# Two blocks of a transformer on one core: modulation chunks reordered at the head of the weight stream, with the first query chunk taken two tiles at a time

## What is computed

```python
c_act = jax.nn.silu(c)
mod = c_act @ w_ada[l] + b_ada[l]
sh_m, sc_m, gt_m, sh_f, sc_f, gt_f = jnp.split(mod, 6, axis=-1)
h = modulate(rms_norm(x, g_mix[l]), sh_m, sc_m)      # h * (1 + sc_m) + sh_m
proj = jnp.einsum('bsd,de->bse', h, w_in[l])
```

## Time and profile before

| | us |
|---|---|
| median of 3 runs | 866.93 (864.98 to 868.29) |
| the profiled execution, its own time | 866.99 |
| its span, first to last instruction | 865.2 |
| TensorE busy | 790.4 (91%) |
| VectorE busy | 683.1 (79%) |
| ScalarE busy | 427.8 (49%) |
| GpSimd busy | 152.8 (18%) |
| mean granted TensorE clock | 0.973 of full speed |
| moved by DMA | 156.93 MB, mean 181 GB/s |

### The profile page before, as it was taken

The page is one execution under the profiler, slowest core; times in us unless marked ns, Lnnn a source line. Parts: engine busy times, 40 slices in busy tenths (PEclk is TensorE's granted clock), DMA queues, the critical chain, the costliest instruction groups (busy, mean ns, idle before and its releaser), DMA issues.

```text
span 865.2 us, 13446 instructions
## 1 busy us (share of the span) xinstructions
PE 790.4 (91%) x5495; PEld 719.0 (83%) x5496; DVE 683.1 (79%) x910; ACT 427.8 (49%) x604; POOL 152.8 (18%) x109
## 2 busy tenths in 40 slices
PE   0599999998989899999998999589979999999996
PEld 0499987886988899999998998468847899999995
DVE  3966477877877799999869899999966955796852
ACT  2444446453645744555445746564446144455652
POOL 0000011221000113211311009975530000000000
PEclk9799999999999999999999999889998999999998
DMA  9976787664745377667645260021220641473201
GB/s 351 401 269 253 276 291 297 228 236 175 240 163 195 107 282 249 241 227 261 248 188 213 81 237 16 40 84 62 67 80 22 236 154 49 172 295 118 98 2 48
DMA packets 26088, 156.93 MB, mean 181 GB/s; under 512 B 2691, under 2 KB 7084, under 8 KB 7852
## 3 DMA queue, kind: packets, MB, share of 16 engines
q1 hardware_dynamic: 21392, 148.91, 46.5%
q10 hardware_dynamic: 4636, 7.18, 2.7%
HBM read 155.01 MB, written 1.06 MB: 180 GB/s over the span
## 4 chain that ended last, share of the span: by engine, by line
PE 68%; DVE 20%; issue 5%; ACT 4%; ACTq 1%; DMA 1%; POOL 0%; DVEq 0%
PE wide L1230 27%; PE bank L1230 26%; DVE arena L1054 6%; DVE w_lo L814 5%; DVE w_lo L844 4%; ACT w_hi L372 2%; PE bank L1501 2%; PE bank L1265 1%; PE wide L1665 1%; PE bank L1641 1%; DMA raw<-in_w 1%; PE bank L1653 1%; PE wide L1329 1%; PE bank L1489 1%; PE bank L1351 1%
## 5 line engine op out<-in xcount | busy, mean ns | idle before, releaser
L844 DVE TENSOR_TENSOR w_lo<-raw,w_hi 128x2048 fp32r<-128x2048 f32 x93 | 215.4, 2318 | 68.1 <-ACT w_hi L372 66.5
L1230 PE MATMUL bank<-h_hi,w_hi 128*128 128x256 f32 x736 | 212.0, 288 | 12.0 <-DVE h_lo L880 9.7
L1230 PE MATMUL bank<-h_lo,w_hi 128*128 128x256 f32 x736 | 209.4, 285 | 0.0
L1230 PE MATMUL bank<-h_hi,w_lo 128*128 128x256 f32 x736 | 209.3, 284 | 0.0
L1230 PE MATMUL wide<-h_hi,w_hi 128*128 128x256 f32 (+1 forms) x576 | 189.2, 329 | 20.7 <-DVE w_lo L844 13.2
L1230 PE MATMUL wide<-h_lo,w_hi 128*128 128x256 f32 (+1 forms) x576 | 185.8, 323 | 0.0
L1230 PE MATMUL wide<-h_hi,w_lo 128*128 128x256 f32 (+1 forms) x576 | 185.7, 322 | 0.0
L372 ACT CAST w_hi<-raw 128x2048 fp32r<-128x2048 f32 x93 | 176.9, 1905 | 10.7 <-DMA raw<-in_w 4.7
L1230 PEld LDWEIGHTS bank<-h_hi,w_hi 128*128 128x128 f32 x736 | 142.2, 193 | 14.3 <-issue 11.3
L1230 PEld LDWEIGHTS bank<-h_lo,w_hi 128*128 128x128 f32 x736 | 142.4, 194 | 0.1
L1230 PEld LDWEIGHTS bank<-h_hi,w_lo 128*128 128x128 f32 x736 | 142.4, 193 | 0.0
(11 more groups left out here) (238 smaller groups left out, 1059.3 us busy)
## 6 DMA issues: line engine op xcount, KB each, us to landing
raw<-in_w SPq DMA_DIRECT2D x141, 1024.0 KB, 4.9
xs<-in_xs ACTq DMA_DIRECT2D x2, 1024.0 KB, 12.9
consts<-diff ACTq DMA_DIRECT2D x8, 128.0 KB, 7.2
cond<-in_cond ACTq DMA_DIRECT2D x1, 1024.0 KB, 7.5
out<-xs SPq DMA_DIRECT2D x4, 256.0 KB, 2.8
consts<-in_c ACTq DMA_DIRECT2D x1, 576.0 KB, 3.9
arena<-in_cond ACTq DMA_DIRECT2D x1, 512.0 KB, 7.0
consts<-in_c ACTq DMA_DIRECT2D x1, 512.0 KB, 3.4
```

The source lines that it names most:

```text
L844: nc.vector.tensor_tensor(w_lo[:, slot, :], raw[:, rslot, :], w_hi[:, slot, :].bitcast(F32), ALU.subtract).then_inc(sem("lo_done"), 1)
L1230: last = mm(out, w[a], x[b], start=start and n == 0, stop=stop and n == 2, skip_group_check=skip)
```

## The change

- The stream begins mod 0, mod 1, lin 0, mod 2 to mod 7, lin 1. Mod chunks now alternate, scale and shift: mod 2n is the scale of tiles 2n and 2n+1, mod 2n+1 their shift. The host arranges weights and biases to match.
- VectorE no longer starts with the remainder of lin 0. It takes mod 0 and 1, then that remainder, and from then on works in four rounds of two tiles: two mod chunks, biases and coefficients of two tiles, `norm_tmp` of two tiles; the `h_lo` of the round before stands between the two mod chunks.
- ScalarE issues `xs`, `c0` and `vec` ahead of `rel` and `onehot`. It takes the squares ahead of the rounded part of lin 0, and the bias row behind the reciprocal root; the three loads of the bias row go behind lin 1's rounded part.
- TensorE begins with 32 products of zeros (128x512, bfloat16), then the sum of squares, then the bias row. Lin 0 is written out: for each tile both halves of the outputs, 6 products, and ahead of tiles 2, 4 and 6 another 16 products of zeros.

```diff
 def stream_order():
-    order = [("lin", 0)] + [("mod", m) for m in range(MOD_FIRST)]
+    order = [("mod", 0), ("mod", 1), ("lin", 0)] + [("mod", m) for m in range(2, MOD_FIRST)]
@@ ScalarE
             act.dma_start(cond_ada, bass.AP(cond_d.tensor, 0, [[0, P], [1, D]])).then_inc(sem("cond_ada_loaded"), 16)
-            act.dma_start(rel[0:32, :], rel_d).then_inc(sem("rel_loaded"), 16)
-            act.dma_start(onehot, c1_d[0:33, 1152:1536]).then_inc(sem("rel_loaded"), 16)
             act.dma_start(xs[:, :, 0:T], xs_d[:, :, 0:T]).then_inc(sem("x_loaded"), 16)
             act.dma_start(c0[:, :], c0_d).then_inc(sem("c0_loaded"), 16)
             act.dma_start(vec[:, :], vec_d).then_inc(sem("vec_loaded"), 16)
+            act.dma_start(rel[0:32, :], rel_d).then_inc(sem("rel_loaded"), 16)
+            act.dma_start(onehot, c1_d[0:33, 1152:1536]).then_inc(sem("rel_loaded"), 16)
...
             act.wait_ge(sem("cond_ada_loaded"), 16)
             nc.scalar.activation(cond_ada, cond_ada, ACT.Silu).then_inc(sem("cond_ada_ready"), 1)
-            split(0)
-
-            act.wait_ge(sem("bias_row"), 1)
-            nc.scalar.copy(urow, bank[3][0:8, 0:384]).then_inc(sem("bias_row_out"), 1)
-            act.wait_ge(sem("bias_row_out"), 1)
-            act.dma_start(diff_d, urow).then_inc(sem("bias_stored"), 16)
-            act.wait_ge(sem("bias_stored"), 16)
...
             act.wait_ge(sem("eps_set"), 2)
             load_ln_exp()
             act.wait_ge(sem("x_loaded"), 16)
             for k in range(KT):
                 square("mix", k)
+            split(0)
             rstd_of("mix")
+            act.wait_ge(sem("bias_row"), 1)
+            nc.scalar.copy(urow, bank[3][0:8, 0:384]).then_inc(sem("bias_row_out"), 1)
+            act.wait_ge(sem("bias_row_out"), 1)
+            act.dma_start(diff_d, urow).then_inc(sem("bias_stored"), 16)
             shift_hi("mix")
@@ VectorE
-            split(0)
+            def mix_lo(n):
+
+                for k in (2 * n, 2 * n + 1):
+                    dve.wait_ge(sem("norm_hi"), k + 1)
+                    nc.vector.scalar_tensor_tensor(h_lo[:, k, 0:T], norm_tmp[:, k, :], norm_shift(ADA_M, k, 0),
+                                                   h_hi[:, k, 0:T].bitcast(F32), ALU.add, ALU.subtract).then_inc(sem("norm_lo"), 1)
...
             dve.wait_ge(sem("cond_ada_ready"), 1)
-            for m in range(MOD_FIRST):
-                mod(m, RAW_OF_MOD[m] % RAW, 16 * (RAW_OF_MOD[m] // RAW + 1), 1, 1)
-            dve.wait_ge(sem("vec_loaded"), 16)
-            mod_bias(0, 8)
-            coefficients(0, "g_mix", mod_row(ADA_SC_M, 0))
-            norm("mix", 1)
+            for n in range(MOD_FIRST // 2):
+                head_mod(2 * n)
+                if n:
+                    mix_lo(n - 1)
+                head_mod(2 * n + 1)
+                if n == 0:
+                    split(0)
+                    dve.wait_ge(sem("vec_loaded"), 16)
+                both, a = modv[:, 8 * n:8 * n + 8].rearrange("p (c v) -> p c v", v=2)[:, :, 0], VEC["mod_bias"] + 8 * n
+                dve.wait_ge(sem("mod_done"), 2 * n + 2)
...
+                if n == 0:
+                    dve.wait_ge(sem("rstd_ready"), 1)
+                dve.wait_ge(sem("mix_coef" if n < 3 else "coef_ready"), n + 1 if n < 3 else 1)
+                for k in (2 * n, 2 * n + 1):
+                    nc.vector.scalar_tensor_tensor(norm_tmp[:, k, :], xs[:, k, 0:T], coef[:, k:k + 1], rstd[:, 0:T],
+                                                   ALU.mult, ALU.mult).then_inc(sem("normed"), 1)
+            mix_lo(3)
             split(1)
@@ TensorE
+            pe.wait_ge(sem("zeros_set"), 1)
+
+            def warm(count):
+
+                for _ in range(count):
+                    mm(wide[:, 3, :], zeros[:, 0:P], zeros[:, :], start=True, stop=True)
+
+            warm(32)
+            pe.wait_ge(sem("c0_loaded"), 16)
+            sum_squares("mix")
...
+            pe.wait_ge(sem("lo_done"), 1)
+            for k in range(KT):
+                if k and k % 2 == 0:
+                    warm(16)
+                tile_ready("mix")(k)
+                for m in range(2):
+                    last = triple(halves(bank[0])[m], whl(0, 256 * k + P * m, P), hhl(k, 0, T), k == 0 and m == 0,
+                                  k == KT - 1, skip=True)
+            last.then_inc(sem("lin_done"), 1)
```

More of the change, by code:

```diff
@@ L1300, in qkv_step @@
                 if n < 4:
[L1301 removed]
+                    features(j, n % SPL, halves(bank[n % 2]), 0, T)
                 else:
@@ L1305, in _ @@
             for i in range(2):
-                for n in range(6):
+                for n in range(0 if i else 1, 6):
                     qkv_step(i, n)
```

43 lines of the change are left out of this document (25 added, 18 removed).

## The result

The changed kernel took **871.91 us** (median, 870.09 to 874.00 in 6 runs) and the kernel before 866.62 in the same comparison. One of the six executions of before took 1562.68 us, and the record shows no reason for it. Without it the median of before is 866.31, so that the change costs 5.6 us; the ratio, which leaves it out too, is **1.0066, 95% interval 1.0041 to 1.0091**. A second comparison, on another chip, gave 871.13 against 866.99, or 4.1 us, and a ratio of 1.0054 with 1.0039 to 1.0069. The forecast was 877.0 within 871.0 to 879.5: the sign and the range held, the size (10.0 us) was nearly twice too large. The time is that of rival 1, worked out as 872.1.

A forecast was written before the change was run, and what follows sets the result against it. VectorE's work was taken to bound the head. Lin 1 starts at X + 7.3 + 0.8 + 21.2 + 4.7 = X + 34.0, against 46.8 before; with X 22.8, 867.0 + 10.0 = 877.0 us, range 871.0 to 879.5.

The forecast's parts named there:

- rival 1: `xs` load: SyncE's queue runs empty, `xs` goes through as before at 17.9 us; 872.1 us, chance 0.25.
- The path: Head: VectorE's work sets when lin 1 can start, and a microsecond there is one at the end.
- VectorE's start: Head: silu stays at 11.4 us, so mod 0 runs from 11.5, a start 1.8 us earlier.
- When `xs` lands: Both DMA queues stay full because the load of 13.9 is there at 14.9; `xs` lands at 22.8 us.
- X: Time at which `xs` lands: 22.8 us in the forecast, 17.9 kept for the range.
- From `xs` to the first `norm_tmp`: Sum of squares and root, or cast and lin 0's remainder: first `norm_tmp` at X + 7.3 us.
- The rounds: VectorE's three rounds behind the first two `norm_tmp`: 7.1 us each, 21.2 in all.
- The end of the head: From the last `norm_tmp`'s slot to lin 1's finished remainder: 4.7 us, unchanged.
- The zeros: Products of zeros on TensorE keep the clock up: worth nothing, at worst 2 to 3 us if it falls at lin 1.
- Rival 3: The clock falls in the rounds or before lin 1; chance 0.10.
- Rival 2: `xs` passes in one go, landing at 11 to 14 us; 867 us, no change; chance 0.07.
- rival 4: Slack further on swallows a part of lin 1's later start; chance 0.03.

The follow-up runs named there:

- e2: Changed kernel with ScalarE's cast of lin 0 back ahead of the squares; 870.99 us against 867.48 for the kernel before, ratio 1.0049.
- e5: Kernel before with only lin 0 taken in both output halves per tile on TensorE, no zeros; 866.75 us against 866.84, ratio 1.0000.
- e12: Changed kernel with `rel` and `onehot` issued ahead of `xs` again; 873.91 us against 867.25 for the kernel before, ratio 1.0081.
- e1: Changed kernel with the loads of `rel` and `onehot` issued behind the silu; 879.81 us against 867.48 for the kernel before, ratio 1.0132.
- e6: Changed kernel without any products of zeros; 873.00 us against 866.84 for the kernel before, ratio 1.0072.
- e3: Changed kernel with the cast ahead of the squares and mod 0 to 3 ahead of the first `norm_tmp`; 869.19 us against 867.48 before, ratio 1.0021.
- e8: e3 without the products of zeros; 868.88 us against 866.84 for the kernel before, ratio 1.0028.
- e7: Kernel before with early silu, mod 0 and 1 ahead of lin 0, squares before bias row, lin 0 in halves; 871.57 us against 866.84, ratio 1.0054.
- e9: e7 with `xs` on SyncE's queue and 48 products of zeros ahead of lin 0; 866.48 us against 866.99 for the kernel before, ratio 0.9996.

## Why the prediction was right or wrong, point by point

**The path: right.** VectorE sets the head, lin 1's remainder is what TensorE waits for, and a microsecond there is one at the end: in three kernels the head moves with the first `norm_tmp`, one for one. It was also right that the new wait is for `xs` and not for the cast (e2), and that lin 0's halves are worth next to nothing (e5).

**VectorE's start: wrong by 1.5 us.** The step was "the same rows are issued before it, in another order, so I leave this as it is". The count is the same but not where the engine is held: behind the 1040 rows of `xs` the issues of `vec` and `rel` took 3.16 and 2.70 us, and the silu ended at 12.93. e12 puts the old order back and has it at 11.57.

**When `xs` lands: wrong, and this is the failed step.** It read "so the load of 13.9 is there at 14.9, before SyncE's queue is empty", from 1.0 us between issue and first row. That figure came from two idle queues. With both queues full it did not hold: e12 issued its load at 14.00 and it was not there at about 15.4, 1.4 us later, where the queue ran empty; e1 issued at 11.65 and was in time at about 15.25. The delay under load is therefore above 1.2 to 1.6 us and at most 3.6. The runs don't narrow it further, and whether it is the queue's turn or a slower issue path that takes this time stays open. In the changed kernel itself the late silu settles it before that: its load was issued at 15.36, too late even with 1.0 us, and first moved at 18.30, when `xs` was through. Either of the two errors was enough by itself to bring `xs` at 18.2. X was 18.24, against 17.9 in rival 1 and 22.8 in the forecast. These 4.6 us are the error of the forecast. I had put the block of a returning queue down as rival 1 with a quarter of the chance because a margin of 0.6 us stood for the other. A margin of that size, resting on a latency measured in another condition, was worth less than 0.55.

That rival 1's 872.1 comes within 0.2 us of the median is in part luck. Its load was to be late by a few tenths, and was late by the silu's 1.5 us as well; its X was 0.3 short, the squares 0.7 short, and the rounds 1.1 too long. The term for the landing, some 0.3 us from the last row to the semaphore, has no row behind it either: by the packets it was 1.1 us in the changed kernel (17.15 to 18.24) and 0.9 in e1 (22.10 to 22.98). So e1's agreement with the 23.0 is that of the whole, with about 0.6 us wrong both ways within it. The semaphore writes, counted as packets like the rest, were short: in before a chunk's 144 packets are 128 of 8 KB, which took 0.31 us each, and 16 of 4 bytes, which took 0.009.

**From `xs` to the first `norm_tmp`: X + 8.0, not X + 7.3.** The sum of squares took 6.39 us where the 5.65 of before was taken. Over all profiles it took 5.2 to 6.7, so the single row was good to a microsecond only, and the term should have had that width. What varies is the moment at which TensorE's pace doubles, behind the first product (see e6).

**The rounds: 6.68 each, not 7.1.** The starts of `norm_tmp` are 26.20, 32.89, 39.57 and 46.25. That is 20.05 us instead of 21.2. Most of it is in the mod chunks: two of them take 4.69 us in a round (27.00 to 29.29 and 30.09 to 32.49) where the 4.97 were taken from chunks that follow one another; the biases and coefficients take 0.40 instead of 0.5. **The end of the head: right.** From the last `norm_tmp`'s slot (47.05) to lin 1's first product (51.85) are 4.8 us against 4.7.

With X = 18.24 the prediction's own sum gives X + 34.0 = 52.2 for lin 1's start; measured is 51.85, from +0.7 for the squares, -1.1 for the rounds and +0.1 for the end. All terms but X together are off by 0.4. One reading was 0.3 off: the 46.8 is the start of ScalarE's copy of lin 0, and lin 1's first product in before starts at 46.52. From there to 51.85 it is 5.3 us, which is the head's 5.4; from 46.8 it would be 5.05.

**The zeros: right in the changed kernel, wrong as a rule for its variants.** e6 leaves them out, and nothing that the times resolve changes. The 32 at the start took 9.98 us, 0.43 each up to 7.23 and 0.22 from there on, and ended 7.52 us before the squares. The clock fell behind them: it was at half from 14.05, and the squares began at 18.82. A block of 16 took 3.63 us at a clock of 1.00. The blocks cost nothing here because TensorE waited longer than a block lasts; in e3 they made lin 0's copy 4.0 us later (49.19 against 45.20 in e8), since there they stand between products that are ready. Rival 3, which set the upper end of the range at 879.5, had two parts, and no run shows a time for either. The clock did fall in the first round of the changed kernel:

```profile
30.00:34.00 4.00, 3.75 (x15) 3.08 (x17) 3.90 (x10) 0.59 (x2) 0.00 (x0) 0.50 0.95 299
```

It cost nothing that shows, since TensorE had ended lin 0 and still waited 2.06 us for lin 1's remainder. The clock down at lin 1 did not come about in this profile; in e2 it did in spite of the zeros, and in e6 and e8 without them. I had no row to tell which.

**The other rivals.** Rival 2, `xs` in one go, is excluded: 244 packets of ScalarE's queue stand against 244 of SyncE's from 10 to 15 us in the trace of the changed kernel. Nothing that shows swallowed the delay (rival 4): the medians moved by 5.6 and 4.1 in the two comparisons, the heads by 5.4 and 5.2.

## What to carry to other kernels

Before moving work on to an input, look at when that input lands and whether anyone waits for it now; a load with 16 us of travel and nobody waiting is a wait in store, and a change that frees stream slots earlier makes it longer (`xs` landed at 18.24, in e1 at 22.98 and in e7 at 28.77). Put an input that must come in time on the same queue as the stream and ahead of the chunks that can wait; that was the edit which turned the head's +5.4 us into +1.5 in the changed kernel and +3.3 into -1.4 in the old order. When two outcomes hang on a few tenths of a microsecond, ask whether the latency in the estimate was measured under the load that will be there; if it was not, give the two the same chance.

## What the runs showed of the hardware

- **Two full queues moved the same number of rows, though one had rows of 8 KB and the other of 1 KB.** 244 to 244 in 5 us of the changed kernel and 91 to 88 in 2 us of e1. So the queue of small rows gets a small share of the bytes (0.25 MB beside 1.85 in those 5 us).
- **A queue that has run empty comes back late while the other is full.** The load of 15.36 first moved at 18.30 (2.9 us), that of 14.00 in e12 at 17.80 (3.8 us), and an issue into idle queues took 1.0 us. From 16 to 18 us ScalarE's queue moved 630 and 652 packets. Which part of the delay is a wait for the other queue's turn is not shown.
- **Issuing a DMA can hold the engine for 3 us.** ScalarE's issue of `vec`, with 128 rows, took 3.16 us and that of `rel` 2.70, behind the 1040 rows of `xs`; the silu behind them was 1.5 us late. With `xs` on another queue (e9) the same issue of `vec` took 0.45. The long issues ended with about the same number of packets of ScalarE's queue still to move: in before, that of `c0` (3.51 us) when 112 of the 1425 issued so far had begun, that of `vec` (2.54 us) at 240 of 1569; in the changed kernel, that of `vec` at 139 of 1472 and that of `rel` at 266 of 1520. So 1254 to 1333 were left. This is what the runs show of the prediction's "room in the queue".
- **Ahead of the first clock record of a trace the view prints 1.00, and the products went at the pace of 0.50.** The 16 products of the sum of squares in before, and in the changed kernel (windows, columns as above):

```profile
22.60:25.60 3.00, 3.00 (x7) 2.46 (x8) 2.79 (x7) 1.99 (x7) 0.00 (x0) 1.00 1.01 403
25.60:28.20 2.60, 2.60 (x10) 1.84 (x9) 2.50 (x5) 0.00 (x0) 0.00 (x0) 1.00 1.05 423
```
```profile
18.80:23.80 5.00, 4.98 (x12) 4.01 (x13) 1.16 (x1) 3.81 (x8) 0.00 (x0) 0.50 0.94 388
23.80:25.20 1.40, 1.40 (x7) 0.93 (x6) 1.36 (x3) 0.00 (x0) 0.00 (x0) 0.82 0.00 0
```

  The first clock record of the trace of before begins at 26.56 us. The products take 0.43 us each up to there (3.00 / 7) and 0.22 from there on, with 1.00 in the view on both sides. In the changed kernel the record is 0.50 from 14.05 until 24.29, and the pace is the same: 0.42 us each up to there, 0.22 from there. That TensorE began the squares of before at half clock too is my estimate from this pace. In all 14 profiles the products go from 0.43 us each to 0.22 at the first record (at 7.23 in the changed kernel, among the zeros, 21.50 in e6, 35.51 in e7). The mean clock of a span counts such a start as full: in before the records at half add up to 46.8 us of the span of 865.2, half of that is 2.7%, and the mean is given as 0.973.
